# Two weight sums of the seven-product down projections, made by transfers from DRAM in three of four feed-forwards

## What is computed

```python
def swiglu_ffn(h, w_up, w_down):
    gate, up = jnp.split(h @ w_up, 2, axis=-1)
    return (jax.nn.silu(gate) * up) @ w_down

for l in range(DEPTH):                    # DEPTH = 2, D_FF = 2816
    x = x + 0.5 * swiglu_ffn(rms_norm(x, norm_ffn1[l]), ffn1_up[l], ffn1_down[l])
    h = rms_norm(x, norm_mix[l])
    ...
    x = x + merged @ w_out[l]
    x = x + 0.5 * swiglu_ffn(rms_norm(x, norm_ffn2[l]), ffn2_up[l], ffn2_down[l])
return rms_norm(x, final_norm)
```

## Time and profile before

| what | us |
|---|---|
| median of 3 runs | 1090.27 |
| lowest, highest run | 1088.67, 1090.99 |
| span of the profiled execution | 1087.6 |

### The profile page before, as it was taken

The page is one execution under the profiler, slowest core; times in us unless marked ns, Lnnn a source line. Parts: engine busy times, 40 slices in busy tenths (PEclk is TensorE's granted clock), DMA queues, the critical chain, the costliest instruction groups (busy, mean ns, idle before and its releaser), DMA issues.

```text
span 1087.6 us, 15436 instructions
## 1 busy us (share of the span) xinstructions
PE 1079.8 (99%) x5308; PEld 906.0 (83%) x5308; DVE 889.0 (82%) x1164; ACT 652.9 (60%) x832; POOL 78.4 (7%) x102
## 2 busy tenths in 40 slices
PE   9999999999999999999999999999999999999997
PEld 6888888988988888888888888888899888888886
DVE  6989988766987698988889988986678777988896
ACT  6656654656953565665565755646469446565664
POOL 0034410100200000000000000001012000000000
PEclk9999999999999999999999999999999999999999
DMA  8576584744455555655646567648444554646651
GB/s 290 178 233 222 169 313 160 253 163 129 159 185 164 173 193 193 204 181 193 220 145 216 180 203 267 235 123 278 140 143 156 193 175 155 221 167 196 221 169 69
DMA packets 140091, 207.38 MB, mean 191 GB/s; under 512 B 5208, under 2 KB 103584, under 8 KB 139536
## 3 DMA queue, kind: packets, MB, share of 16 engines
q1 hardware_dynamic: 137600, 197.15, 54.8%
q0 software_dynamic: 2144, 9.12, 2.4%
q10 hardware_dynamic: 304, 0.53, 0.1%
HBM read 205.60 MB, written 1.05 MB: 190 GB/s over the span
## 4 chain that ended last, share of the span: by engine, by line
PE 98%; DVE 1%; DMA 0%; SPq 0%; ACT 0%; issue 0%
PE psum L1694 31%; PE psum L1696 31%; PE psum L1695 31%; PE psum L1793 2%; PE psum L1712 1%; PE psum L1981 1%; DMA x<-x_dram 0%; PE psum L1995 0%; SPq L487 0%; PE psum L2028 0%; DVE xT L1078 0%; PE psum L2030 0%; DVE w_lo L1078 0%; DVE xs L1181 0%; ACT xT L704 0%
## 5 line engine op out<-in xcount | busy, mean ns | idle before, releaser
L1078 DVE TENSOR_TENSOR w_lo<-raw,w_hi 128x1024 fp32r<-128x1024 f32 (+6 forms) x279 | 412.2, 1503 | 76.2 <-ACT w_hi L689 75.3
L1694 PE MATMUL psum<-w_hi,xT 128*128 128x512 f32 (+2 forms) x984 | 383.1, 389 | 0.1
L1696 PE MATMUL psum<-w_hi,xT 128*128 128x512 f32 (+2 forms) x984 | 379.3, 385 | 0.0
L1695 PE MATMUL psum<-w_lo,xT 128*128 128x512 f32 (+2 forms) x984 | 378.9, 385 | 0.0
L689 ACT ACTIVATE w_hi<-raw 128x2048 fp32r<-128x2048 f32 (+5 forms) x167 | 284.5, 1710 | 72.0 <-PE psum L1696 66.8
L1694 PEld LDWEIGHTS psum<-w_hi,xT 128*128 128x128 f32 x984 | 184.7, 188 | 40.5 <-DVE w_lo L1078 1.9
L1696 PEld LDWEIGHTS psum<-w_hi,xT 128*128 128x128 f32 x984 | 184.7, 188 | 37.1
L1695 PEld LDWEIGHTS psum<-w_lo,xT 128*128 128x128 f32 x984 | 184.9, 188 | 34.3 <-issue 0.2
L806 ACT ACTIVATE oT<-xs 128x1024 fp32r<-128x1024 f32 x72 | 76.5, 1063 | 69.9 <-DVE xs L1078 69.9
L774 ACT ACTIVATE scores<-psum,stat 128x256 f32<-128x256 f32 x88 | 41.1, 472 | 110.5 <-PE psum L1696 109.7
L1078 DVE TENSOR_TENSOR oT<-xs,oT 128x1024 fp32r<-128x1024 f32 x72 | 88.0, 1229 | 0.0
(11 more groups left out here) (221 smaller groups left out, 1413.7 us busy)
## 6 DMA issues: line engine op xcount, KB each, us to landing
raw<-ffn_up_dram SPq DMA_DIRECT2D x170, 512.0 KB, 4.9
raw<-ffn_down_dram SPq DMA_DIRECT2D x44, 1024.0 KB, 4.9
raw<-w_in_dram SPq DMA_DIRECT2D x20, 1024.0 KB, 5.3
raw<-w_attn_proj_dram SPq DMA_DIRECT2D x8, 1024.0 KB, 5.0
raw<-w_out_dram SPq DMA_DIRECT2D x8, 1024.0 KB, 5.3
raw<-w_uq_dram SPq DMA_DIRECT2D x8, 576.0 KB, 4.0
gates<-b_gate_dram POOLq DMA_DIRECT2D x4, 1024.0 KB, 7.5
raw<-w_ukv_dram SPq DMA_DIRECT2D x8, 512.0 KB, 4.0
```

The lines of the kernel that those rows point to most:

```text
L1078: return dve.tensor_tensor(dst, a, b, ALU.subtract)
L1694: nc.tensor.matmul(dst, a_hi, b_hi, start=first, stop=False)
L1695: nc.tensor.matmul(dst, a_hi, b_lo, start=False, stop=False)
L1696: return nc.tensor.matmul(dst, a_lo, b_hi, start=False, stop=last)
```

## The change

In the feed-forwards after the very first, T1 and T3 are no longer added by VectorE. The signs are turned so that the sums are plain ones: T1 = B11 + B12, T3 = B12 + B22, T2 = B22 + T1, T4 = B21 + T2, with S1 = A21 - A22 and S4 = A12 + S2 on the hidden side, and -0.5 for 0.5 where two of the results enter `x`. SyncE loads B11 and B12 into `tsum` (`load_base`), GpSimd waits until they have landed and issues a transfer that adds B12 and B22 from DRAM to them (`sum_weights`), and VectorE waits for that one in `addB_first`.

```diff
+            def load_base(L, f, d):
+                if L or f:
+                    if isinstance(d, int):
+                        sp.wait_ge(norm_lo.sem, norm_lo.upto(L, QUARTERS * (2 * f)))
+                    else:
+                        sp.wait_ge(sumB_lo.sem, sumB_lo.upto(L, (f * SEVEN + d) * 2 - 1))
+                    sp.dma_start(tsum[:, 0:2 * N512], downs[f][L, bass.ds(d * CH, P), :]).then_inc(base_landed, 16)
...
                 load_down(L, f, q0 + 1, 1, 0)
-                with nc.sync.Fori(2, NCH) as j:
+                load_base(L, f, 0)
+                with nc.sync.Fori(2, NCH - 1) as j:
                     load_up(L, f, q0 + j - 1, 2, j, 0)
                     load_up(L, f, q0 + j, 0, j, 1)
                     load_seven(L, f, q0 + j, j - 1)
+                    load_base(L, f, j - 1)
...
+            def sum_weights(L, f):
+                for d in range(SEVEN):
+                    pool.wait_ge(base_landed, 16 * summed(L, f, d))
+                    right = downs[f][L, d * CH:(d + 1) * CH, N512:D].rearrange("(k p) n -> p k n", p=P)
+                    pool.dma_start(tsum[:, 0:2 * N512].rearrange("p (k n) -> p k n", k=KCH), right,
+                                   accum_op=ALU.add).then_inc(sums_landed, 16)
...
             def rest(L):
+                if L:
+                    sum_weights(L, 0)
...
                 norm_rsqrt(L, 2)
+                sum_weights(L, 1)
...
             def addB_first(L, f, d):
+                if L or f:
+                    dve.wait_ge(sums_landed, 16 * summed(L, f, d))
+                    dve.sem_inc(sumB_step.sem, 1)
+                    return
...
-                minus(tsum[:, 0:2 * N512].rearrange("p (c n) -> p c n", c=2), b[:, :, 1, :],
-                      b[:, 0, :, :]).then_inc(sumB_step.sem, 1)
+                dve.tensor_tensor(tsum[:, 0:2 * N512].rearrange("p (c n) -> p c n", c=2), b[:, :, 1, :],
+                                  b[:, 0, :, :], ALU.add).then_inc(sumB_step.sem, 1)
```

More of the change, by code:

```diff
@@ L282, in trunk @@
         sumB_hi, sumB_lo = event("sumB_hi", 2 * 2 * SEVEN), event("sumB_lo", 2 * 2 * SEVEN)
+        base_landed, sums_landed = sem("base_landed"), sem("sums_landed")
         m1_copied, joined = event("m1_copied", 2), event("joined", 2 * 8)
@@ L338, in half, with summed @@
             return slice(h * N512, (h + 1) * N512)
+        def summed(L, f, d):
+            return (2 * L + f - 1) * SEVEN + d + 1
         def part_count(p, part):
@@ L507, in ffn @@
                     load_seven(L, f, q0 + j, j - 1)
+                    load_base(L, f, j - 1)
+                j = NCH - 1
+                load_up(L, f, q0 + j - 1, 2, j, 0)
+                load_up(L, f, q0 + j, 0, j, 1)
+                load_seven(L, f, q0 + j, j - 1)
                 load_down(L, f, q0 + NCH - 1, 2, NCH - 1)
@@ L1319, in addA @@
                     dve.wait_ge(sumA_lo.sem, sumA_lo.upto(L, f * SEVEN + d))
-                dve.tensor_tensor(tile(S1), tile(A21), tile(A22), ALU.add)
+                minus(tile(S1), tile(A21), tile(A22))
                 minus(tile(S3), tile(A11), tile(A21)).then_inc(sumA_step.sem, 1)
@@ L1324, in addA @@
                 dve.wait_ge(sumA_step.sem, sumA_step.upto(L, n + 2))
-                minus(tile(S4), tile(A12), tile(S2)).then_inc(sumA_step.sem, 1)
+                dve.tensor_tensor(tile(S4), tile(S2), tile(A12), ALU.add).then_inc(sumA_step.sem, 1)
             def sumA(L, f, d):
@@ L1348, in addB_second @@
                 dve.wait_ge(sumB_step.sem, sumB_step.upto(L, n + 1))
-                minus(quad(tsum, T2), quad(raw[:, 1, :], B22), quad(tsum, T1)).then_inc(sumB_step.sem, 1)
+                dve.wait_ge(raw_landed[1], (L * (GROUPS // RING + 2 * UPS[1]) + f * FFN2_0 // RING + d + (f + 1) * UPS[1]) * 16)
+                dve.tensor_tensor(quad(tsum, T2), quad(raw[:, 1, :], B22), quad(tsum, T1), ALU.add).then_inc(sumB_step.sem, 1)
                 dve.wait_ge(sumB_step.sem, sumB_step.upto(L, n + 2))
-                minus(quad(tsum, T4), quad(raw[:, 1, :], B21), quad(tsum, T2)).then_inc(sumB_step.sem, 1)
+                dve.tensor_tensor(quad(tsum, T4), quad(raw[:, 1, :], B21), quad(tsum, T2), ALU.add).then_inc(sumB_step.sem, 1)
             def addB(L, f, d):
@@ L1367, in sumB, with into_x @@
                     sumB_half(L, f, d, i)
-            def into_x(L, f, n, t, h, src, after):
+            def into_x(L, f, n, t, h, src, after, factor=0.5):
                 if after:
                     dve.wait_ge(joined.sem, joined.upto(L, 8 * f + after))
-                mul_add(x[:, t, half(h)], src, 0.5, x[:, t, half(h)]).then_inc(joined.sem, 1)
+                mul_add(x[:, t, half(h)], src, factor, x[:, t, half(h)]).then_inc(joined.sem, 1)
             def join_first(L, f):
@@ L1382, in join_first @@
                 dve.tensor_tensor(u3, psum[:, 7, :], u2, ALU.add).then_inc(joined.sem, 1)
-                into_x(L, f, 4, 0, 1, u2, 2)
+                into_x(L, f, 4, 0, 1, u2, 2, -0.5)
             def join_second(L, f):
@@ L1387, in join_second @@
                 into_x(L, f, 6, 0, 1, psum[:, 5, :], 4)
-                into_x(L, f, 7, 1, 1, u3, 3)
+                into_x(L, f, 7, 1, 1, u3, 3, -0.5)
                 into_x(L, f, 8, 1, 1, psum[:, 5, :], 7)
```

## The result

| | median of runs, us | span of the profiled execution, us |
|---|---|---|
| before | 1090.05 | 1087.6 |
| changed | 1133.51 (1131.87 to 1134.32) | 1130.1 |

The ratio is 1.040, with a 95% interval from 1.0387 to 1.0413. The change costs 43.5 us, where 18 were forecast. The time lies within the range of 1098 to 1150 and next to rival 1 (1132), in part by luck, as the last sections show.

The account below looks back on a forecast made before the run. TensorE was taken to bound the kernel; chunk 0 of three feed-forwards adds 18.0 us, steady chunks and the rest 0, so 1090.3 + 18.0 = 1108.3, say 1108 us. Range 1098 to 1150.

Parts of the forecast that it names:

- rival 1: Steady chunks: accumulate collides with up loads, takes about 8.8 us, loop 16.9 us; 1132 us; chance 0.27 to 1150, 0.09 above.
- What bounds the kernel: Whole kernel: TensorE, busy 99%, bounds it; work off VectorE is worth only TensorE's waits for it, 2.7 us.
- The signs: Sign changes put `add` for `subtract` and -0.5 for 0.5 in instructions of the same shape: nothing.
- The new instructions on GpSimd stand where it has nothing else to do ...: nothing: GpSimd's queue: it is busy only 78.4 us and its root of the norm stays ahead, so the additions cost nothing.
- Chunk 0: Start of three feed-forwards: the base waits for the norm, the sum delays VectorE's split; 5.8, 6.4 and 5.8 us, sum 18.0.
- The steady loop: 24 steady chunks: from sum landing through additions, base and accumulate to the next sum, costing 0, but barely.
- Sum: 15.6 us against a period of 16.14. The loop fits with 0.5 us to spare: Steady chunks: additions 1.42 and 1.22, SyncE 0.25, base 5.1, waking 0.1, accumulate 7.5, within TensorE's period.
- the point of 8.0 us: Steady chunks: the accumulate may take 8.0 us before each chunk grows by the excess.
- the choice of 7.5 us: Accumulating 512 KB transfer priced like GpSimd's 1024 KB transfer, 7.5 us, with 10 for the range.
- 3.2 us of traffic: Steady accumulate carrying twice its bytes: 3.2 us of traffic last 6.5 with half of the DMA engines.
- the one row of doubled traffic: Profile row of a 1024 KB transfer from GpSimd beside the steady loads, 7.5 us, taken for the 512 KB accumulate.
- also ran beside such loads: Argument against the collision in steady chunks: the 7.5 us transfer row was itself measured beside such loads.

Follow-up runs that it names:

- e6: Changed kernel with sums by transfers only in the two second feed-forwards, started early in two slots of `gates`, VectorE adding elsewhere: 1091.08 us, ratio 1.0012.
- e7: Changed kernel with the turned signs alone, all T1 and T3 added by VectorE, no new transfers or waits: 1089.89 us, ratio 1.0002.
- e2: Changed kernel with GpSimd's second-layer bias broadcasts put between the last sums again instead of behind all nine: 1126.65 us, ratio 1.0345.
- e3: Changed kernel with a plain copy in place of the accumulating transfer, same queue, bytes and waits, result differs: 1103.3 us, ratio 1.0128.
- e1: Changed kernel with chunk 0's T1 and T3 added by VectorE again in all feed-forwards, chunks 1 to 8 by transfers: 1120.15 us, ratio 1.0285.
- e4: Changed kernel with looped chunks' up weight loads bringing a quarter of their bytes, result differs: 1109.07 us, ratio 1.0173.
- e5: Changed kernel with 18 idle products put where TensorE waits in chunk 0 of the three feed-forwards: 1131.92 us, ratio 1.0388.

## Why the prediction was wrong in size

**What bounds the kernel.** Right: TensorE bounds it, and VectorE's relief brings nothing. e6 shows it for 20 of the 31 us, with 18 sums in time.

**The signs and GpSimd's other work.** The signs are free (e7). The step "The new instructions on GpSimd stand where it has nothing else to do ...: nothing" failed. I asked whether GpSimd was free for the new instructions, and not what would start late behind them. Its broadcasts for the mixer aren't urgent themselves, but 2.8 MB of them set free at once collided with loads that are. That is 6.3 us in the profiled execution, 6.9 in e2. Both were to be read in the trace of before: when the broadcasts ran, and how often up loads follow.

**Chunk 0.** Forecast 18.0 us. In the three traced starts TensorE is 19.5 us late, a good match, but in part by chance. Base and accumulate together were faster than priced: 3.4 and 8.1 us in the first start, 4.4 and 5.6 in the second, 3.2 and 7.5 in the third, that is 11.5, 10.0 and 10.7 for 12.4. "DMA: Bandwidth & Descriptors" in the Trainium skill (anatomy of one DMA) has a fixed part plus bytes for transfers from GpSimd, 3.2 us here by estimate. That is near the first base, though SyncE issues it, and half of what the plain copy of e3, which GpSimd issues, took beside other loads, 6.0. The half clock after the wait, up to 2.6 us a start, wasn't in the sum; the two errors work against each other. The first start is also no fixed amount: in e2's trace it cost 3.2 us between the first two marks for 7.2. And in the median time removing the starts gives only 13.4 us (e1), since the loop takes the rest: the two places aren't independent sums, as they were treated.

**The steady loop.** The step that failed is "Sum: 15.6 us against a period of 16.14. The loop fits with 0.5 us to spare". Its mechanism was right, and so nearly was the point of 8.0 us from which it decides (7.8 with the measured other terms). The term that was mis-sized is the accumulate: the choice of 7.5 us put the loop on the wrong side of that point. Measured against forecast: accumulate 8.5 for 7.5; base with GpSimd's waking 5.5 for 5.2; landing to VectorE 0.24, which was left out; SyncE 0.03 for 0.25; the additions 1.33 for 1.42. That is 16.84, 0.7 over the period, and up to 18.0 in other turns (958.04 to 976.00 us). Rival 1 gave 16.9 from an accumulate of 8.8 us, and 1132 us. It rested on doubled traffic times shared engines. No row of before shows its "3.2 us of traffic"; e4's 3.3 us bear it out. The forecast used the one row of doubled traffic (7.5 us for 1024 KB) as if it held both. That the row "also ran beside such loads" was a weak argument. In the second layer those broadcasts were issued behind both pairs of up loads:

```profile
657.66 0.59 POOL L527 DMA_DIRECT2D gates<-b_gate_dram  x1 [101.84 <-ACT w_hi L801]
```

The pairs began at 654.00 and 656.18 us. The accumulate at 431.95 comes between its pairs, at 431.16 and 433.58. e3 and e4 show that both factors are there, and either one alone leaves the loop within its period. Rival 1's total, though, is near by luck: it put 20 us on the steady loop and 22 on the starts, against 16.7 and 19.5 in the trace, and nothing on the last interval, which took 6.3.

**Sum of it.** In the medians, 43.5 us. e2 takes out 6.9, e1 13.4; some 23 us are left for the loop, if the two add up, which was not run together. e3, whose loop fits, is 13.8 us over before, and that with shorter starts and a shorter end than the changed kernel's.

## What to carry to other kernels

Work moved off an engine that has slack is worth nothing, and it turns a local dependency into a round trip: before doing so, add up the loop from "buffer free" to "buffer free again" (issue, landing, wake-up, the second transfer, first use) and compare it with the period of the engine that bounds. If the loop is within a microsecond of the period, price each link by its worst neighbour, not its median, or give it a second buffer and an earlier start, as e6 does. And when instructions are put into a queue, ask what starts late behind them and what that then collides with, even if nobody waits for it.

## What the runs showed of the hardware

- A transfer that adds into SBUF held the DMA engines 1.8 times as long as a copy of the same 512 KB (3.3 us in e4, 1.8 in e3). Beside 2 MB of other loads a chunk it landed in 8.5 us for the copy's 6.0; with a quarter of those loads beside it, in 6.2.
- GpSimd took 1.19 us to issue an accumulate (431.95 above) and 0.72 us to issue the copy in e3 (the first row below).
- The other loads pay too. In the changed kernel the up loads issued at 433.58 and 434.13 us, behind the accumulate, land in 8.0 and 8.8 us. Before, the second pair of such a chunk (442.79 and 443.35 us) landed in 4.9 and 5.8.
- After 4.5 us without work TensorE ran at half clock for 5.7 us, after 3.7 us in each of the second and third starts for about 5.6 and 3.4 us, in the third only from some 0.7 us after it had begun again. 18 idle products in the wait keep the clock at 1.00 in all three starts (e5).
- The length of the wait alone doesn't tell whether the clock falls: it stayed full after 3.1 us in e2, and was at half after 2.5 us in e4, whose rows stand below (the wait, then the stretch behind it). What else decides is not shown here.

```profile
426.73 0.72 POOL L655 DMA_DIRECT2D xs<-ffn_down_dram  x1 [14.71 <-DMA xs<-ffn_down_dram]
...
384.32 0.19 PEld L1732 LDWEIGHTS psum<-w_hi,xT 128*128 128x128 f32 x1 [2.52 <-DVE w_lo L1111]
...
384.80:388.20 3.40, 3.40 (x10) 2.63 (x9) 3.24 (x8) 1.10 (x2) 0.00 (x0) 0.50 0.29 77
```
